# Two access patterns in the expert rounds of a decoder trunk: interleaved stationary parts, and down weights stored and read in reverse

## What is computed

```python
def swiglu(h, wg, wu, wd):
    return (jax.nn.silu(h @ wg) * (h @ wu)) @ wd

def moe_swiglu(h, router_w, wg, wu, wd):
    ...
    gates = jnp.sum(jax.nn.one_hot(top_idx, N_EXPERTS, dtype=jnp.float32) * top_w[..., None], axis=1)
    y = jnp.zeros_like(hf)
    for e in range(N_EXPERTS):
        y = y + gates[:, e:e + 1] * swiglu(hf, wg[e], wu[e], wd[e])
```

## Time and profile before

| | |
|---|---|
| median of 3 runs | 1452.6 us (1450.4 to 1453.82) |
| span of the profiled execution | 1453.1 us |
| PE busy | 1426.3 us (98%) |
| PEld busy | 1202.9 us (83%) |
| DVE busy | 1179.7 us (81%) |
| ACT busy | 884.7 us (61%) |
| chain that ended last | PE 78%, DVE 11%, DMA 3% |

### The profile page before, as it was taken

The page is one execution under the profiler, slowest core; times in us unless marked ns, Lnnn a source line. Parts: engine busy times, 40 slices in busy tenths (PEclk is TensorE's granted clock), DMA queues, the critical chain, the costliest instruction groups (busy, mean ns, idle before and its releaser), DMA issues.

```text
span 1453.1 us, 22261 instructions
## 1 busy us (share of the span) xinstructions
PE 1426.3 (98%) x8381; PEld 1202.9 (83%) x8381; DVE 1179.7 (81%) x1181; ACT 884.7 (61%) x879; POOL 141.4 (10%) x195
## 2 busy tenths in 40 slices
PE   8999999999999999999999999999999999999997
PEld 6887888999998888887888888888888888888875
DVE  7998886676467697876988988889898898898896
ACT  5334754534344345644768768777777777777774
POOL 1910100000000000101960000000000000000100
PEclk9999999999999999999999999999999999999999
DMA  7443445776455442454999999999999999999993
GB/s 285 136 180 121 156 159 189 261 246 233 151 189 192 174 160 97 151 188 161 365 413 390 406 363 399 380 364 413 353 398 394 354 404 370 379 397 347 419 376 145
DMA packets 94247, 408.87 MB, mean 281 GB/s; under 512 B 28769, under 2 KB 43233, under 8 KB 47714
## 3 DMA queue, kind: packets, MB, share of 16 engines
q1 hardware_dynamic: 75984, 391.37, 69.9%
q10 hardware_dynamic: 17042, 12.36, 2.6%
q0 software_dynamic: 1152, 4.19, 0.7%
HBM read 390.98 MB, written 14.16 MB: 279 GB/s over the span
## 4 chain that ended last, share of the span: by engine, by line
PE 78%; DVE 11%; DMA 3%; SPq 3%; issue 2%; ACT 2%; POOL 1%; DVEq 0%; POOLq 0%; ACTq 0%
PE psum L1938 25%; PE psum L1940 24%; PE psum L1939 24%; DVE w_lo L605 4%; SPq L696 3%; PE psum L1954 2%; DMA w_raw<-in_stream 2%; DMA x_normed<-y_rows,row_number 1%; ACT w_hi L599 1%; ACT square_out L993 0%; PE psum L2284 0%; PE psum L2005 0%; DVE s_r L1511 0%; ACT prob L1129 0%; PE psum L1987 0%
## 5 line engine op out<-in xcount | busy, mean ns | idle before, releaser
L605 DVE TENSOR_TENSOR w_lo<-w_raw,w_hi 128x2048 fp32r<-128x2048 f32 x267 | 607.9, 2293 | 130.2 <-ACT w_hi L599 129.4
L599 ACT ACTIVATE w_hi<-w_raw 128x2048 fp32r<-128x2048 f32 x267 | 509.4, 1915 | 251.1 <-PE psum L1940 191.5
L1938 PE MATMUL psum<-w_hi,hsT_hi 128*128 128x512 f32 x448 | 176.0, 393 | 0.8 <-DVE hsT_lo L1829 0.8
L1940 PE MATMUL psum<-w_lo,hsT_hi 128*128 128x512 f32 x448 | 174.5, 390 | 0.0
L1939 PE MATMUL psum<-w_hi,hsT_lo 128*128 128x512 f32 x448 | 174.3, 389 | 0.0
L1938 PE MATMUL psum<-w_hi,hT_hi 128*128 128x512 f32 x376 | 152.7, 406 | 1.8 <-ACT gate_ssm L1075 1.4
L605 DVE TENSOR_TENSOR w_lo_more<-w_raw,w_hi_more 128x2048 fp32r<-128x2048 f32 x56 | 128.2, 2289 | 24.3 <-ACT w_hi_more L599 23.6
L1940 PE MATMUL psum<-w_lo,hT_hi 128*128 128x512 f32 x376 | 147.4, 392 | 0.0
L1939 PE MATMUL psum<-w_hi,hT_lo 128*128 128x512 f32 x376 | 147.1, 391 | 0.0
L599 ACT ACTIVATE w_hi_more<-w_raw 128x2048 fp32r<-128x2048 f32 x56 | 107.1, 1913 | 21.6 <-DMA w_raw<-in_stream 12.4
L1938 PE MATMUL psum<-hT_hi,w_hi 128*128 128x256 f32 x416 | 116.6, 280 | 0.2 <-DVE hT_lo L1463 0.2
(11 more groups left out here) (429 smaller groups left out, 2651.2 us busy)
## 6 DMA issues: line engine op xcount, KB each, us to landing
w_raw<-in_stream SPq DMA_DIRECT2D x323, 1024.0 KB, 6.9
w_raw_more<-in_stream SPq DMA_DIRECT2D x40, 1024.0 KB, 7.7
h_rows<-one_row ACTq DMA_DIRECT2D x10, 512.0 KB, 6.6
round_rows<-h_rows SPq DMA_DIRECT2D x7, 512.0 KB, 7.0
y_rows<-y_slots ACTq DMA_DIRECT2D x7, 512.0 KB, 9.2
y_rows<-one_row ACTq DMA_DIRECT2D x4, 512.0 KB, 6.2
gain_row<-in_gain_rows SPq DMA_DIRECT2D x3, 512.0 KB
x_tok<-in_x SPq DMA_DIRECT2D x2, 512.0 KB, 6.2
```

What stands on the lines that cost most here:

```text
L599: nc.scalar.activation(split_of(seg, i)[0], raw_of(seg, i), ACT.Copy).then_inc(s_hi, 1)
L605: nc.vector.tensor_tensor(l_, raw_of(seg, i), h.bitcast(F32), ALU.subtract).then_inc(s_lo, 1)
L1938: mm(out, lh, rh, start=start, stop=False)
L1940: return mm(out, lh, rl, start=False, stop=stop)
```

## The change

The high and low parts of the gathered rows become one tensor, `hsT_parts`, of 128 x 8 x 128 x 2, in the same 8192 bytes. `hsh` is every even element of it and `hsl` every odd one. So a stationary block of 128 columns is read with a step of two elements (8 bytes), ACT writes its high part and DVE reads it and writes the low part with the same step. The layout of `eactT_hi` and `eactT_lo` stays; only the spelling of their operands changes.

The host turns each run of 512 elements in the expert rounds' down slots around (`backwards`), and the moving operand of the down matmuls, high part and low, is read from its last element to its first, a step of minus one. DMA, ACT's copy and DVE's subtraction of these slots stay as they are. The dense layer's down slots (`ffn_slot`) are not touched.

```diff
-        hsh = at("hsT_hi", [P, KD, P], F32R, a_k)
-        hsl = at("hsT_lo", [P, KD, P], F32R, a_k + 4096)
+        hs2 = at("hsT_parts", [P, KD, P, 2], F32R, a_k)
+        hsh, hsl = hs2[:, :, :, 0], hs2[:, :, :, 1]
...
             def hs_lo(g):
-                V.tensor_tensor(hsl[:, 4 * g:4 * g + 4, :].rearrange("p k n -> p (k n)"), bank(2 + g),
-                                hsh[:, 4 * g:4 * g + 4, :].rearrange("p k n -> p (k n)").bitcast(F32),
+                V.tensor_tensor(hsl[:, 4 * g:4 * g + 4, :], bank(2 + g).rearrange("p (k n) -> p k n", n=P),
+                                hsh[:, 4 * g:4 * g + 4, :].bitcast(F32),
                                 ALU.subtract).then_inc(s_hsf, 1)
...
-                    V.tensor_tensor(bTl[:, j % 2, 0:n // P].rearrange("p k n -> p (k n)"), bank(4 + t % 2)[:, 0:n],
-                                    bTh[:, j % 2, 0:n // P].rearrange("p k n -> p (k n)").bitcast(F32),
+                    V.tensor_tensor(bTl[:, j % 2, 0:n // P], bank(4 + t % 2)[:, 0:n].rearrange("p (k n) -> p k n", n=P),
+                                    bTh[:, j % 2, 0:n // P].bitcast(F32),
                                     ALU.subtract).then_inc(s_trf[t % 2], 1)
...
-                            m = mm3(bank(c), bTh[:, j % 2, kk, :], bTl[:, j % 2, kk, :], H[:, k, c * 512:(c + 1) * 512],
-                                    L[:, k, c * 512:(c + 1) * 512], start=(d == 0 and k == 0),
+                            m = mm3(bank(c), bTh[:, j % 2, kk, :], bTl[:, j % 2, kk, :], H[:, k, c * 512:(c + 1) * 512][:, ::-1],
+                                    L[:, k, c * 512:(c + 1) * 512][:, ::-1], start=(d == 0 and k == 0),
...
+def backwards(slot):
+
+    return slot.reshape(P, SLOT // 512, 512)[:, :, ::-1].reshape(P, SLOT)
...
 def round_slot(gate, up, down, what):
     kind, j, h = what
     if kind == "d":
-        return slot_of(down, 2 * j, 2, 0, D)
+        return backwards(slot_of(down, 2 * j, 2, 0, D))
```

## The result

The changed kernel takes 1471.9 us, median of four runs (1469.8 to 1472.9); the kernel before, beside it, 1452.4. The ratio is 1.0133, 95% interval 1.0118 to 1.0147: slower by some 19.5 us. The likeliest case of the prediction, no change, did not come; the range of 1449 to 1481 holds the time, because it reached up to rival 2.

The account below looks back on a forecast made before the run. The prediction took PE, busy without idle time in the expert rounds, to bound the kernel. It summed 1453.1 us for the profiled execution plus four terms of 0, named 1453.0 us, and gave a range of 1449 to 1481 us.

Parts of the forecast that it names:

- likeliest case: Whole kernel: no change, 1453.0 us, with its own range of 1450 to 1456; 71%.
- rival 2: Expert-round matmuls: load outgrows its cover (19 us) or backward start costs a little (14 us); typical 1470, together 1486; 9%.
- What bounds the kernel: Expert rounds: PE-bound, no idle time; each nanosecond of step worth 2.1 us (gathered rows) or 1.1 us (down weights).
- The sum: Whole kernel: profiled execution of 1453.1 us plus four terms of 0 gives 1453.1, named as 1453.0.
- Part 1: Stationary gathered rows read with a step of two, 2112 matmuls: cost 0, bounds 0 to 19 us.
- Part 2: Moving down weights read backwards, 1056 matmuls: cost 0; half rate would be 230 us, a dearer start 14 us.
- dearer start: Backward down matmuls: only the start costs more, bounded by 13 ns each over 1056 matmuls, 14 us.
- Parts 3 and 4: ACT's copy and DVE's subtraction writing with step two, and unchanged DMA, weight split and waits: cost 0; writers 10 us at most.

Follow-up runs that it names:

- whole runs: Against the kernel before: interleaved stationary rows alone, 1465.7 us, ratio 1.0087; backward reading of the down weights alone, 1460.3 us, ratio 1.0050.
- The table: Mean steps from two matmul-only programs over moving widths, plain, strided and backward; the backward toll is 7 to 9 ns at 512 and 510 columns, nothing from 320 down.
- The trace of the patterns: Matmuls alone, 48 of each operand pattern, the kernel's computation left out; at 512 columns 227 ns plain, 233 with a stationary step of two, 233 backward.
- the last program: Matmuls alone at 510 to 480 columns, plus other banks, bfloat16 and stationary steps of 1 to 4; plain 512 columns 226.7 ns, bfloat16 215.8 ns.

## Why the prediction was right or wrong

**What bounds the kernel: right.** PE without idle time, so that each nanosecond of step is worth 2.1 or 1.1 us. This carried what followed: 6.9 ns x 2112 = 14.6 us and 7.0 ns x 1056 = 7.4 us, measured in whole runs as 13.6 and 8.2. One thing did hide part of it, though the prediction says that nothing does: in the last round PE had 1.6 us of waits to lose, so seven rounds of the eight paid. The sum also set a span, 1453.1 us, beside a median of times; a time is 1.8 us above its span (1471.55 against 1469.8 after), so that execution was some 2 us above the median, which changes nothing in the outcome.

**Part 1, the stationary step of two: wrong in its value.** The bounds of 0 to 19 us held the 13.6, but I took 0, "because a load has over 100 ns of cover at 512 columns". The load was even shorter than I allowed for, 118 ns at most, and it cost all the same. The step that failed is the thought that an operation with cover costs nothing. The step of 227 ns holds 13 ns that are not columns, and I had shown only that a smaller load doesn't shorten them at 256 columns, not that another load doesn't lengthen them at 512. The table shows how weak a witness the 256-column rows were: at that width both patterns cost nothing.

**Part 2, the backward read: wrong in its value.** The bound for a dearer start, 13 ns or 14 us, held 8.2; I took 0 on the ground of equal density. A gap between neighbours makes the large cost (453 ns with a step of two); equal density did not rule out the small one.

**Parts 3 and 4: right but for one wait.** DVE's 684 ns stayed. ACT's copy took 59 ns more, some 0.1 us a round, and no PE wait came of it. Counts are as they were. "No wait is added or removed" was wrong by the 1.6 us for which PE waited for `eactT_lo` in the last round: they are gone in the changed kernel.

**The range and the rivals.** Rival 2 came, both of its halves together, at 1472 against "typical 1470". For both together it named 1486, above the range's end of 1481; the time fell inside only because each toll was smaller than its bound, 13.6 us instead of 19 and 8.2 instead of 14. That the range holds is luck in this respect. The mechanism for the load was wrong as well: it was to decide when a load takes over 227 ns, and that never happened. It had 9% where no change had 71%. With two new patterns on the bottleneck and no row that showed either, two terms set to 0 were the weak point, and their bounds, 1467 to 1486, were the better forecast. The range held the time; the likeliest case, which set both terms to 0, did not.

**The rule for strides.** The trace of the patterns departs from the Trainium skill, "SBUF — State Buffer", section "SBUF: two separate sides": by it four fp32 can be strided for free. A moving operand with a step of two ran at 453 ns instead of 227, and a stationary one with a step of four was recorded with loads of 310 ns instead of 188. The measurement decides. For the two patterns of the change, full rate within a line is right to 3% of the step at 512 columns, and 3% was the question.

## What to carry to other kernels

Where PE never idles, the access pattern of its operands is part of the bottleneck, even when it moves the same bytes and even on the side that has cover. Keep both operands of a 512-column fp32r matmul plain and at the start of a line; a stationary step of two or a backward moving operand costs 3% of the step, a moving step of two doubles it. Before an unseen pattern is set to zero, multiply a few nanoseconds by the count: 6.4 ns by 3168 matmuls is 20 us here, of which 18 came through.

## What the hardware showed that was not expected

- The 226.7 ns step of 512 fp32r columns is a favourable case: 510 columns take 226.7 as well, 508 take 227.8, and half the stationary columns make it slower (230.0). bfloat16 operands take 215.8 in every pattern.
- The moving side pays in full for a gap between neighbours at once (453 ns for a step of 2, 461 for 4), the stationary side only from a step of three on: at 128 moving columns and the full clock there is a matmul every 112 ns with step 1, 118 with step 2, 173 with step 3, 234 with step 4 and 240 with step 8.
- While loads took that long, the clock fell as well: with one 128-column matmul per 240 ns it went to the 1.2 GHz level though PE was never recorded idle. In the last program it did the same during the steps of three and of four.
```profile
216.00:221.70 5.70, 5.70 (x51) 5.70 (x50) 0.00 (x0) 0.00 (x0) 1.00 0.00 0
221.70:233.00 11.30, 11.30 (x49) 11.30 (x49) 0.00 (x0) 0.00 (x0) 0.62 0.00 0
233.00:243.50 10.50, 10.50 (x50) 10.50 (x51) 0.00 (x0) 0.00 (x0) 0.50 0.01 2
```
  (Columns: window, length, busy and count of PE, PEld, ACT and POOL, granted clock, DMA share, GB/s.)
